# The down product of a feed-forward layer in seven chained products, with eight operand sums in place of ten

## The reference

```python
def swiglu(h, w_gate, w_up, w_down):
    return (jax.nn.silu(h @ w_gate) * (h @ w_up)) @ w_down

x = x + 0.5 * swiglu(rmsnorm(x, ffn1_norm), ffn1_w_gate, ffn1_w_up, ffn1_w_down)
x = x + mixer(rmsnorm(x, mix_norm))
x = x + cross_attention(rmsnorm(x, mem_q_norm), rmsnorm(mem, mem_kv_norm))
x = x + 0.5 * swiglu(rmsnorm(x, ffn2_norm), ffn2_w_gate, ffn2_w_up, ffn2_w_down)
y = rmsnorm(x, final_norm)
```

## Time and profile before

| | |
|---|---|
| time, median of 3 runs | 2225.29 us (2223.29 to 2226.63) |
| the profiled execution | 2222.05 us, span 2220.3 us, granted TensorE clock 0.961 |
| busy share of the span | PE 92%, DVE 68%, POOL 49%, ACT 41% |
| largest share of the chain that ended last | PE 35%, DVE 9% |
| first down part | from about 478 to 724 us of the span |
| second down part | from about 1956 to 2198 us of the span |

### The profile page before, as it was taken

One profiled execution on the slowest core, in us unless ns is written; L12 is line 12 of the kernel. 1 busy time (PEld: TensorE's weight loads), 2 busy tenths in 40 slices (PEclk: granted clock), 3 DMA queues, 4 the chain that ended last, 5 costly groups with the idle time before them and its releaser, 6 DMA issues. The chain is left out here.

```text
span 2220.3 us, 26577 instructions
## 1 busy us (share of the span) xinstructions
PE 2038.5 (92%) x9585; PEld 1682.9 (76%) x9585; DVE 1509.7 (68%) x1825; ACT 912.0 (41%) x1606; POOL 1082.8 (49%) x822
## 2 busy tenths in 40 slices
PE   4899999999998899887889999994999999999996
PEld 3688888877766689677778888873888888877775
DVE  7756565559999632599955555567565656569997
ACT  6443433334444311466634444434434343334443
POOL 3555555548698121287811100125555555468782
PEclk7899999999999999989899999996999999999998
DMA  3222223262400131332134432130222222263201
GB/s 114 76 76 89 82 73 91 75 228 89 148 19 1 62 110 61 95 86 58 44 97 126 126 91 60 57 95 19 81 90 76 86 86 74 67 229 105 105 1 76
DMA packets 217499, 190.24 MB, mean 86 GB/s; under 512 B 7532, under 2 KB 173976, under 8 KB 217368
## 3 DMA queue, kind: packets, MB, share of 16 engines
q1 hardware_dynamic: 217280, 188.51, 27.6%
q10 hardware_dynamic: 88, 0.02, 0.0%
HBM read 152.85 MB, written 35.65 MB: 85 GB/s over the span
## 5 line engine op out<-in xcount | busy, mean ns | idle before, releaser
L1734 DVE TENSOR_TENSOR w_lo<-st,w_hi 128x512 fp32r<-128x512 f32 x176 | 192.4, 1094 | 200.7 <-ACT w_hi L1314 200.1
L922 PE MATMUL ps<-T_hi,w_lo 128*128 128x512 f32 x704 | 278.4, 395 | 48.5 <-DVE T_lo L1734 47.7
L922 PE MATMUL ps<-tr_hi,sr_lo 128*128 128x512 f32 x616 | 249.5, 405 | 36.2 <-DVE tr_lo L1734 32.9
L923 PE MATMUL ps<-T_lo,w_hi 128*128 128x512 f32 x704 | 276.7, 393 | 0.0
L924 PE MATMUL ps<-T_hi,w_hi 128*128 128x512 f32 x704 | 276.3, 392 | 0.0
L923 PE MATMUL ps<-tr_lo,sr_hi 128*128 128x512 f32 x616 | 243.1, 395 | 0.0
L924 PE MATMUL ps<-tr_hi,sr_hi 128*128 128x512 f32 x616 | 242.9, 394 | 0.0
L922 PE MATMUL ps<-B_hi,w_lo 128*128 128x512 f32 x528 | 207.7, 393 | 8.7 <-DVE w_lo L1734 6.3
L807 POOL TENSOR_TENSOR ssum<-piece_A 128x512 f32<-128x512 f32 x110 | 180.5, 1643 | 69.1 <-DVE sr_lo L1734 67.6
L923 PE MATMUL ps<-B_lo,w_hi 128*128 128x512 f32 x528 | 207.3, 393 | 0.0
L924 PE MATMUL ps<-B_hi,w_hi 128*128 128x512 f32 x528 | 207.3, 393 | 0.0
(11 more groups left out here) (228 smaller groups left out, 4937.1 us busy)
## 6 DMA issues: line engine op xcount, KB each, us to landing
gate_raw<-in_ffn_w_gate SPq DMA_DIRECT2D x44, 512.0 KB, 5.2
up_raw<-in_ffn_w_up SPq DMA_DIRECT2D x44, 512.0 KB, 5.1
h_spill<-up_s SPq DMA_DIRECT2D x66, 256.0 KB, 2.0
piece_A<-in_ffn_w_down SPq DMA_DIRECT2D x32, 512.0 KB, 5.0
piece_B<-h_spill SPq DMA_DIRECT2D x32, 512.0 KB, 4.9
wa_raw<-in_w_in SPq DMA_DIRECT2D x16, 512.0 KB, 4.0
wb_raw<-in_w_out SPq DMA_DIRECT2D x16, 512.0 KB, 4.1
wb_raw<-in_mem_w_kv SPq DMA_DIRECT2D x16, 512.0 KB, 3.8
```

The source lines that it names most:

```text
L922: pe.matmul(to, w_lo, m_hi, start=first, stop=False, skip_group_check=joins)
L923: pe.matmul(to, w_hi, m_lo, start=False, stop=False, skip_group_check=joins)
L1734: return dve.tensor_tensor(to, value, plain(hi), ALU.subtract)
```

## The change

The down part takes another form of the seven products, the chained one that the gate and up part uses already. Three of the seven products (1, 5 and 2) open a PSUM bank; the other four are added by TensorE onto a bank that an earlier product has left there. Each bank is added to x when a product has ended, but now to one place each, with the factor 0.5: 7 additions per tile position in place of 12, 56 in place of 96 of a down part. The bank is not cleared by the addition.

The operands are eight sums per slot, 88 of a feed-forward: S1 = A21 + A22, S2 = A22 - S3, S3 = A11 - A21, S4 = A12 - S2, T1 = B12 - B11, T2 = B22 - T1, T3 = B22 - B12, T4 = B21 - T2. All are made by DVE (`sums`, two steps ahead of their use, and `sum_s3`, three steps behind product 1). S2, S3 and T1 overwrite blocks in place (A21, A11, B11), T2 has a tile of its own (`t2`), the other four go through a ring of three (`sum_ring`). POOL has no more work in the down steps; the sums of squares for the first norm, which it made among them, come behind that loop.

With this go: the order of the products (1, 5, 6, 3, 7, 2, 4, and 4 before 2 in the second half), the order and the place of the block loads, four buffers for the right operand's parts in place of three, the banks of the groups (`group_of`, `on_group`), additions one step later (except group 11), and the steps at which the norm's and the output's work stand.

```diff
-        tr_hi = at(48, "tr_hi", [P, 3, HALF], F32R)
-        tr_lo = at(54, "tr_lo", [P, 3, HALF], F32R)
-        ssum = at(60, "ssum", [P, 2, HALF])
-        tsum = at(64, "tsum", [P, 3, HALF])
+        tr_hi = at(48, "tr_hi", [P, 4, HALF], F32R)
+        tr_lo = at(56, "tr_lo", [P, 4, HALF], F32R)
+        sum_ring = at(64, "sum_ring", [P, 3, HALF])
...
-        PRODUCTS = (4, 2, 7, 1, 5, 3, 6)
...
+        PRODUCTS = (1, 5, 6, 3, 7, 2, 4)
+        USES = {1: ("A11", "B11", "A21"), 5: ("A21", "A22", "B12", "B11"), 6: ("A22", "A11", "B22", "B11"),
+                3: ("A12", "A21", "B22"), 7: ("A11", "B22", "B12"), 2: ("A12", "B21"), 4: ("A22", "B21")}
+        INTO = {1: (0, 1), 5: (1, 0), 6: (0, 0), 3: (0, 0), 7: (1, 0), 2: (0, 1), 4: (1, 1)}
+        OPENS = (1, 5, 2)
...
-            for i, M_ in enumerate(PRODUCTS):
+            for i, M_ in enumerate(PRODUCTS if kh == 0 else PRODUCTS[:5] + (4, 2)):
...
+        LEAD, S3_LAG = 2, 3
...
+        product_of = [steps2[first_of[g]][1] for g in range(14)]
+        group_of = [(g // 7 + (product_of[g] in (5, 3, 2))) % 2 for g in range(14)]
+        on_group = [max([h for h in range(g) if group_of[h] == group_of[g]], default=None) for g in range(14)]
 
         def bank2(g, j):
-            return j if g % 2 == 0 else 4 + (j + 1) % 4
+            return j if group_of[g] == 0 else 4 + (j + 1) % 4
...
-            g = max([g for g in range(13) if last_of[g] + 3 <= e], default=None)
+            g = max([g for g in range(13) if last_of[g] + (3 if g == 11 else 4) <= e], default=None)
...
                 sp.wait_ge(p1_done, nth_product(r, last, 1))
-                whole(r, "A22")
+                whole(r, "A11")
                 sp.wait_ge(p1_done, nth_product(r, last, 6))
-                whole(r, "B21")
+                whole(r, "B11")
+                sp.wait_ge(p1_done, nth_product(r, last, 7))
+                whole(r, "A21")
                 store(r, PAIRS - 1, "c11")
                 sp.wait_ge(p1_done, nth_product(r, last, 2))
-                whole(r, "B11")
...
+                whole(r, "A22")
+                sp.wait_ge(p1_done, nth_product(r, last, 5))
+                whole(r, "B12")
+                whole(r, "B22")
                 store(r, PAIRS - 1, "c21")
                 whole(r, "A12")
...
-            for c in range(DC):
-                sum_squares(3, c)
+            for q in range(2, 4):
+                for c in range(DC):
+                    sum_squares(q, c)
...
-                    if k == 0 and g >= 2:
-                        pe.wait_ge(p2_add, added(r, g - 2, j))
+                    if k == 0 and on_group[g] is not None:
+                        pe.wait_ge(p2_add, added(r, on_group[g], j))
...
-                          tr_hi[:, e % 3, :], tr_lo[:, e % 3, :], k == 0, k == KH[kh] - 1).then_inc(p2_step, 1)
+                          tr_hi[:, e % 4, :], tr_lo[:, e % 4, :], k == 0 and p in OPENS, k == KH[kh] - 1,
+                          p not in OPENS).then_inc(p2_step, 1)
...
-                    if r == 0 and e == 70:
+                    if r == 0 and e == 68:
                         norm_tot(2)
-                    if r == 0 and e == 73:
+                    if r == 0 and e == 72:
                         norm_bc(2)
-                    if r == 1 and e == 67:
+                    if r == 1 and e == 66:
                         y_turn(0)
                         y_turn(1)
-                    if r == 1 and e == 75:
+                    if r == 1 and e == 74:
                         y_turn(2)
                         y_turn(3)
...
+            def sums(r, e):
+                _, p, kh, slot, _ = steps2[e]
+                if p == 5:
+                    b11, b12 = piece["B11"][:, slot, :], raw_piece(r, "B12", kh, slot)
+                    dve.wait_ge(p2_lo, used_by(r, 1, kh, slot))
+                    dve.tensor_tensor(b11, b12, b11, ALU.subtract).then_inc(p2_sum, 1)
+                    a21, a22 = raw_piece(r, "A21", kh, slot), raw_piece(r, "A22", kh, slot)
+                    dve.wait_ge(p2_lo, ring_free(r, "S1", kh, slot))
+                    dve.tensor_tensor(in_ring("S1", kh, slot), a21, a22, ALU.add).then_inc(p2_sum, 1)
...
+            def sum_s3(r, e):
+                _, p, kh, slot, _ = steps2[e]
+                if p == 1:
+                    a21 = raw_piece(r, "A21", kh, slot)
+                    a11 = piece["A11"][:, slot, :]
+                    dve.wait_ge(p2_lo, used_by(r, 1, kh, slot))
+                    dve.tensor_tensor(a11, a11, a21, ALU.subtract).then_inc(p2_sum, 1)
...
                 for e in range(3, STEPS):
+                    if e + LEAD < STEPS:
+                        sums(r, e + LEAD)
                     split_lo(r, e)
+                    sum_s3(r, e - S3_LAG)
                     behind(e)
```

More of the change, by code:

```diff
@@ new lines, in layer_program @@
+        made_at, ring_at, ring_read = {}, {}, []
+        for e in range(3, STEPS):
+            if e + LEAD < STEPS:
+                _, p, kh, slot, _ = steps2[e + LEAD]
+                for what in {5: ("T1", "S1"), 6: ("S2", "T2"), 3: ("S4",), 7: ("T3",), 4: ("T4",)}.get(p, ()):
+                    made_at[what, kh, slot] = len(made_at) + 1
+                    if what in ("S1", "S4", "T3", "T4"):
+                        ring_at[what, kh, slot] = len(ring_at)
+                        ring_read.append(2 * (e + LEAD) + (1 if what[0] == "S" else 2))
+            _, p, kh, slot, _ = steps2[e - S3_LAG]
+            if p == 1:
+                made_at["S3", kh, slot] = len(made_at) + 1
@@ new lines, in layer_program, with p2_made, in_ring, ring_free @@
+        MADE = len(made_at)
+        def p2_made(r, what, kh, slot):
+            return MADE * r + made_at[what, kh, slot]
+        def in_ring(what, kh, slot):
+            return sum_ring[:, ring_at[what, kh, slot] % 3, :]
+        def ring_free(r, what, kh, slot):
+            n = ring_at[what, kh, slot]
+            return 2 * STEPS * r + ring_read[n - 3] if n >= 3 else 2 * STEPS * r
+        def used_by(r, p, kh, slot):
+            return 2 * (STEPS * r + [x[1:4] for x in steps2].index((p, kh, slot)) + 1)
@@ new lines, in side_a @@
+        def side_a(r, e):
+            _, p, kh, slot, _ = steps2[e]
+            if p in (1, 2, 4):
+                name = {1: "A11", 2: "A12", 4: "A22"}[p]
+                return piece[name][:, slot, :], landed(r, name, kh, slot)
+            what = {5: "S1", 6: "S2", 3: "S4", 7: "S3"}[p]
+            at_ = (piece["A21"][:, slot, :] if p == 6 else piece["A11"][:, slot, :] if p == 7
+                   else in_ring(what, kh, slot))
+            return at_, (p2_sum, p2_made(r, what, kh, slot))
@@ L302, in landed, with side_b @@
+        def side_b(r, e):
+            _, p, kh, slot, _ = steps2[e]
+            if p in (1, 2, 3):
+                name = {1: "B11", 2: "B21", 3: "B22"}[p]
+                return piece[name][:, slot, :], landed(r, name, kh, slot)
+            what = {5: "T1", 6: "T2", 7: "T3", 4: "T4"}[p]
+            at_ = (piece["B11"][:, slot, :] if p == 5 else t2[:, slot, :] if p == 6
+                   else in_ring(what, kh, slot))
+            return at_, (p2_sum, p2_made(r, what, kh, slot))
         def landed(r, name, kh, slot):
@@ L307, in landed @@
             return p2_in[name][2], 16 * (3 * r + (1 if slot == 5 else 2 if kh else 0) + 1)
-        TILE_ORDER = {12: (2, 0, 1, 3)}
+        TILE_ORDER = {12: (1, 0, 2, 3)}
         ADDS_2 = []
         for g in range(14):
[L312 to L317, removed]
+            ADDS_2.append([(j, INTO[steps2[first_of[g]][1]]) for j in TILE_ORDER.get(g, range(4))])
         adds_before = [sum(len(a) for a in ADDS_2[:g]) for g in range(15)]
@@ L649, in ffn_loads @@
                     for name in BLOCKS:
[L650 removed]
+                        used = [g for g in range(7) if name in USES[PRODUCTS[g]]]
                         slot = e - first_of[used[-1]]
```

190 lines of the change are left out of this document (77 added, 113 removed).

## The result

The changed kernel takes 2159.53 us (median of 4 runs, 2158.99 to 2162.35) against 2224.29 (2222.95 to 2226.63) of the kernel before side by side on one chip: a ratio of 0.9713, 95% interval 0.9701 to 0.9726, so 64.8 us or 2.9% faster. The forecast was 2161, inside 2151 to 2186. Its profiled execution took 2162.35 us, span 2160.6, granted TensorE clock 0.965.

What follows compares the result with a forecast made beforehand. DVE, slowed by POOL's sums, was taken to bound the down parts; gains of 31.9 and 26.9 us in them plus 3.1 and 2.7 behind make 64.6, giving 2161 us, range 2151 to 2186.

Steps and rivals of the forecast that it cites:

- DVE's price: Down parts: with POOL silent a big DVE instruction costs 0.60 us, so 298 take 178.8 us per part.
- DVE's mean price (2295): Rival: today's 0.95 and 0.91 us per instruction are DVE's own, so 48 more make it slower, 2295 us; chance 0.05.
- the record's 0.68 as price (2179): Rival: each DVE instruction costs its full record, 9.1 us of wait per part in the heavy steps, 2179 us; chance 0.12.
- TensorE becomes the bound: Down parts: DVE falls below TensorE's 209.5 us, so parts take 213.8 and 214.5 us, gaining 31.9 and 26.9.
- the floors: Down parts: 77 steps x 12 matmuls x 0.2267 us plus norm or output work, 211.6 us first, 213.4 second.
- The ledger: Count of DVE's instructions by step against TensorE's 2.72 us: wait about 1.0 us at steps 9 and 10, none at 39 to 52.
- starting lead: Step 2: its low part is ready 2.1 us before TensorE needs it, DVE owing five instructions.
- Group 12 on group 11: Product 4 opens on banks product 7 just filled: costs 1.2 us (0 to 2.4) in the first part, 0.1 in the second.
- the landing rival: Rival: first pieces land late, about 3 us of wait and 5.4 of low clock per part, 2177 us; chance 0.05.
- Start and landing: Part start: TensorE starts step 0 0.23 us after its last matmul, not 0.69; waits for landings stay hidden, 2 us spare.
- The rival with a lead of 2 at step 67 in both parts (2172): New order waits: group 12 waits 4 us per part, final rows and norm's factor may be late, 2172 us; chance 0.09.
- Behind the parts: After each part's last matmul: last additions to x start sooner, gaining 3.1 us after the first part, 2.7 after the second.

Runs made afterwards that it cites:

- old_form_dve: The kernel before with its ten sums per slot made by DVE instead of POOL; 2192.63 us, ratio 0.9867 against the kernel before.
- new_form_pool: The changed kernel with its eight sums moved to POOL and the first norm's sums of squares put back among them; 2198.14 us.
- new_form_pool_noise: The changed kernel with POOL making one sum that nobody reads in each of steps 3 to 58; 2196.32 us.
- light_22_c: The changed kernel with 22 idle DVE subtractions more per part, one in each of steps 14 to 35, where DVE has room; 2161.67 us.
- heavy_22: The changed kernel with 22 idle DVE subtractions more per part, in steps 3 to 10 and 39 to 52, without room; 2185.02 us.
- again_c: The changed kernel as it is, run once more beside the two adds_sooner kernels; 2161.56 us, ratio 0.9717 against the kernel before.
- adds_sooner_c: The changed kernel with the additions of group 11 behind the low parts of step 66 instead of 67; 2159.07 us.
- adds_sooner_lead1_c: As adds_sooner_c, with the operand sums made one step ahead of use instead of two; 2155.85 us against again_c's 2161.56.

## Why the prediction was right

**DVE's price (right).** 298 instructions at 0.60 instead of 250 at a mixed 0.95: DVE's sums start 0.60 apart, old_form_dve and new_form_pool trace it to POOL's presence, and new_form_pool_noise produces it in the changed kernel, with DVE's work left as it was. That settles two rivals. The one with DVE's mean price (2295) is out: no group of the 298 averages over 0.8 us. The one with the record's 0.68 as price (2179) is out too: the rows have starts at 490.27 and 490.87 with records of 0.68. The rule weighed beside it, of the Trainium skill, VectorE: DVE Perf Modes, "The DRAIN you can't avoid", is that the next instruction does not start until the pipeline has emptied; the same section adds that a next one which is not held starts earlier. By the 0.60 between starts the second sentence fits these instructions, and the prediction had weighed the first alone. The other rule weighed, the Trainium skill's Perfetto Trace Analysis, "Optimizing Scalar/DVE Operations", is that moving work off a saturated DVE, even to GpSimd, may make sense. In new_form_pool such a move costs 38.6 us, though from a DVE that was no longer the bound; old_form_dve makes the opposite move off POOL onto a DVE busy for 97% of the part and gains 30. The section's own reservation, that between these two it might not help, is the part that holds.

**TensorE becomes the bound (right).** Losses over the floors were 34.1 and 28.0 us; they are 218.5 - 211.6 = 6.9 and 215.9 - 213.4 = 2.5. The forecast had 2.2 and 1.1. The next two points hold the difference; the norm's and the output's work within the parts took 0.3 and 0.4 us less than the floors allow for. Two of the prediction's signs were missed by the same token: the windows were to be 213 to 216 us and the first is 218.5, and DVE was to be busy for some 85% and is so for 91% and 87%. The 178.8 us behind the 85% leave out what else DVE does in a part (the last hidden values, the norm or the output): 198.1 - 178.8 = 19.3 us in the first, with the few instructions that POOL's squares stretch.

**The ledger (right in place, short in size).** TensorE waits at steps 9 and 10, as counted. But the starting lead was 0.6, not 2.1: DVE owed seven instructions up to the low part of step 2 where five had been counted, three of them for the last hidden values, so that it was done at 483.1 and due at 483.7. With +0.3 and three times -0.3 the lead is gone at step 6 instead of 9; steps 7 and 8 then lose 0.3 each and 9 and 10 lose 0.85, with slower restarts 2.3 us in all in either part, not 1.0. The second half's heavy steps show no wait, as counted; light_22_c and heavy_22 confirm the ledger's shape.

**Group 12 on group 11 (right mechanism, size wrong in the first part).** This is the term that was mis-sized most: 1.2 us, with bounds 0 to 2.4, measured 4.5, outside the bounds. In the second part, where POOL is silent, the same place loses 0.3 (forecast 0.1), so a lead of about 6 us is reached when nothing disturbs it. In the first part the forecast set POOL's stretching against DVE's slack over steps 63 to 71 as a whole. The bank is due in the middle of that stretch: three of the slow low parts (3 x 1.1 = 3.3 us) come before it, and the slack of the steps behind it comes too late. The low part of step 67 is done at 659.8 and due at 663.1, a lead of 3.3 where 6.0 was counted, which accounts for the wait's 2.9. The rest, 1.5 us, is the low clock behind the wait, eight matmuls 0.2 late. The prediction knew such a cost from the start of the part before (5.4 us at 484 to 496) but put it only on the landing rival, and it read it too large. PE in the kernel before, then the window of its first slow matmuls:

```profile
483.77 0.50 PE L922 MATMUL ps<-tr_hi,sr_lo 128*128 128x512 f32 x1 [2.05 <-DVE tr_lo L1734]
...
490.52 0.51 PE L922 MATMUL ps<-tr_hi,sr_lo 128*128 128x512 f32 x1 [2.13 <-DVE tr_lo L1734]
```
```profile
484.11:487.48 3.37, 3.37 (x10) 2.59 (x8) 3.27 (x4) 1.40 (x3) 3.37 (x3) 0.51 1.03 355
```

The 12 us hold a second wait, 2.13 us before step 2, which makes 2.3 of the 5.4; matmuls at the low clock make 3.2, behind two waits of 2 us. The prediction had also written that waits at step 65 for x would prove it wrong; one did occur, in the first part alone, and it took 4.5 of 60 us.

**Start and landing (right).** Step 0 follows in 0.23 us, no wait ends in a DMA. The landing rival (2177) is out.

**Other order waits.** The rival with a lead of 2 at step 67 in both parts (2172) happened by half, in one part, and without its other members: neither the final rows nor the norm's factor made TensorE wait.

**Behind the parts (right, and a little more).** The additions behind the first part start even 0.9 us before its end (they were 3.4 behind it), and 3.0 us are gained against 3.1. For the second part the rows of the changed kernel, DVE and then PE:

```profile
2142.56 2.47 DVE L1920 SCALAR_TENSOR_TENSOR xT<-ps,xT 128x512 f32<-128x512 f32 x4
```
```profile
2145.09 3.71 PE L1093 MATMUL ps<-ident,xT 128*128 128x128 f32 x32 [3.02 <-DVE xT L1920]
```

The last 32 transposes start 3.2 us after the part's end instead of 5.9: the 2.7 forecast. They also take 3.71 us where the kernel before took 5.88 for the same 32, and that was not forecast. The same row of the kernel before, with its window:

```profile
2203.40 5.88 PE L1086 MATMUL ps<-ident,xT 128*128 128x128 f32 x32 [5.74 <-DVE xT L1880]
```
```profile
2203.40:2209.28 5.88, 5.88 (x32) 5.64 (x32) 1.04 (x7) 3.16 (x6) 0.00 (x0) 0.62 0.00 0
```

The granted clock was 0.62 after 5.74 us of idle time; in the changed kernel it is 1.00 over these transposes, behind 3.02 us. Of these 4.9 us (2.7 and 2.2), 0.8 go again in the final rows' work behind (11.8 us against 11.0). The shorter idle time does not explain this by itself: behind the same 3.02 us the 32 transposes took 3.71 us in again_c, adds_sooner_c and light_22_c too, but 5.38 in adds_sooner_lead1_c, 5.21 in heavy_22, 6.54 in new_form_pool and 5.38 in new_form_pool_noise. So the 2.2 us do not come with the earlier start by themselves, and what decides over them is open.

## What to carry to other kernels

When two engines contend, price an instruction by its record beside a silent neighbour and beside a busy one; moving work onto the fuller engine can then empty it. Removing uncontended instructions from a pair that contends can give back much less than their time (12.5 us for 80 additions here, two executions). For an engine that runs in order, count its instructions by step against the consumer's pace, and put a disturbance against the slack that is there before its due time, not against the slack of a whole stretch; a wait of 2 to 3 us can cost some 1.5 us more in clock.

## What the runs showed of the hardware

- One POOL sum of 128x512 with both inputs in SBUF costs DVE more than half a microsecond, whatever it is for: 0.52 as noise. As an estimate, against a reckoning of DVE at 0.60 per big instruction and 198.1 - 298 x 0.60 = 19.3 us for the rest, it is (238.4 - 250 x 0.60 - 19.3) / 110 = 0.63 in the kernel before, and (218.0 - 210 x 0.60 - 19.3) / 88 = 0.83 in new_form_pool.
- A DVE instruction with one input in PSUM is untouched by this: 677 to 678 ns where POOL makes sums all along the part (the kernel before, new_form_pool, new_form_pool_noise), and 677 to 686 where it does not.
- Sums in place cost the same as sums to another tile: 682 ns for both.
- The length of a wait alone did not decide whether TensorE's granted clock fell. It fell to about half after waits of 2.05 and 2.13 us (the kernel before, at 483.77 and 490.52) and of 2.71 and 2.69 us (the changed kernel and again_c, before step 65), within two matmuls in three of these cases and in the changed kernel only behind five matmuls at full pace (660.57 to 661.80). After 3.02 us ahead of the last transposes these took 3.71 us in four kernels (1.00 in the changed one) and 5.2 to 6.5 us in four others. After waits of at most 1.2 us (heavy_22 and adds_sooner_c) it did not fall.
